# Head norms taken in the next head's turn, x loaded first, and latent attention with keys and values ahead of queries in the first pair

## The reference

```python
def hgrn_layer(h, mix, a, lb, w_in, g_out, w_out):
    q, f, i, g = jnp.split(h @ w_in, 4, axis=-1)
    ...
    o, S = mix(a, heads(jax.nn.silu(q)), heads(k), heads(i), heads(log_forget))
    o = rmsnorm(o, g_out.reshape(HG_HEADS, HG_DV)).reshape(Bn, T, -1).astype(h.dtype)
    return (o * jax.nn.silu(g)) @ w_out, S

# trunk, for each layer l
x = x + 0.5 * mods[:, 0, 2] * swiglu(mod(x, 0), w_ffn_gu[l, 0], w_ffn_down[l, 0])
y = hgrn_layer(...) if l == 0 else mla_layer(...)
x = x + mods[:, 1, 2] * y
x = x + 0.5 * mods[:, 2, 2] * swiglu(mod(x, 2), w_ffn_gu[l, 1], w_ffn_down[l, 1])
# before layer 1: ckv, krope = shared_kv(x, ...)
# mla_layer: qc = rmsnorm(h @ w_dq); q_lat, q_rope from qc; scores against ckv and krope; softmax; values; w_out
```

## Time and profile before

| what | before |
|---|---|
| median of 3 runs | 2585.49 us (2585.37 to 2586.11) |
| profiled execution: its own time, its span | 2586.55 us, 2585.0 us |
| busy share of the span: PE, PEld, DVE, ACT, POOL | 93%, 88%, 48%, 25%, 2% |
| mean granted clock of TensorE | 0.961 |
| head turns 0 to 6 (from 503.71 us to 807.60) | 303.9 us |
| last head (807.60 to 884.0) | 76.4 us |
| output projection (884.0 to 934.5) | 50.5 us |

### The profile page before, as it was taken

The page is one execution under the profiler, slowest core; times in us unless marked ns, Lnnn a source line. Parts: engine busy times, 40 slices in busy tenths (PEclk is TensorE's granted clock), DMA queues, the critical chain, the costliest instruction groups (busy, mean ns, idle before and its releaser), DMA issues.

```text
span 2585.0 us, 45686 instructions
## 1 busy us (share of the span) xinstructions
PE 2402.6 (93%) x19640; PEld 2270.4 (88%) x19640; DVE 1232.3 (48%) x2232; ACT 655.0 (25%) x810; POOL 53.9 (2%) x78
## 2 busy tenths in 40 slices
PE   5999999899997699999999999999787779999999
PEld 4999999898986599999998999998666459999998
DVE  4443344465657754434455443545554325543443
ACT  3222122222223122211233221123333223221213
POOL 2000000000000000000000000000000100000000
PEclk7999999899999699999999999999898989999999
DMA  7443452434333134434433443312112412323322
GB/s 258 164 163 111 136 164 81 145 116 132 115 132 107 34 114 165 146 100 151 133 98 123 158 150 102 98 62 71 63 38 90 167 78 82 98 70 101 91 73 74
DMA packets 317308, 294.42 MB, mean 114 GB/s; under 512 B 15597, under 2 KB 290116, under 8 KB 316144
## 3 DMA queue, kind: packets, MB, share of 16 engines
q1 hardware_dynamic: 310928, 260.41, 31.2%
q0 software_dynamic: 6240, 31.98, 3.3%
HBM read 284.83 MB, written 7.51 MB: 113 GB/s over the span
## 4 chain that ended last, share of the span: by engine, by line
PE 88%; DVE 6%; ACT 3%; issue 1%; DMA 1%; SPq 0%; DVEq 0%; ACTq 0%
PE ps L689 24%; PE ps L691 24%; PE ps L690 24%; PE ps L720 3%; PE ps L966 2%; PE ps L1252 1%; PE ps L1273 1%; ACT w_hi L1388 1%; DMA xs<-in_x_sample 1%; PE ps L1294 1%; DVE rstd L2107 1%; PE ps L1222 1%; PE ps L1203 1%; PE ps L1002 1%; DVE w_lo L1783 1%
## 5 line engine op out<-in xcount | busy, mean ns | idle before, releaser
L689 PE MATMUL ps<-hn_hi,w_hi 128*128 128x260 f32 (+1 forms) x2608 | 764.3, 293 | 14.1 <-DVE w_lo L1783 5.7
L691 PE MATMUL ps<-hn_hi,w_lo 128*128 128x260 f32 (+1 forms) x2608 | 747.8, 287 | 0.0
L690 PE MATMUL ps<-hn_lo,w_hi 128*128 128x260 f32 (+1 forms) x2608 | 747.6, 287 | 0.0
L1783 DVE TENSOR_TENSOR w_lo<-raw,w_hi 128x2048 fp32r<-128x2048 f32 (+5 forms) x200 | 381.0, 1907 | 345.0 <-ACT w_hi L1388 344.6
L689 PEld LDWEIGHTS ps<-hn_hi,w_hi 128*128 128x128 f32 x2608 | 500.5, 192 | 32.1 <-issue 23.6
L690 PEld LDWEIGHTS ps<-hn_lo,w_hi 128*128 128x128 f32 x2608 | 502.2, 193 | 0.1
L691 PEld LDWEIGHTS ps<-hn_hi,w_lo 128*128 128x128 f32 x2608 | 500.1, 192 | 0.0
L1388 ACT ACTIVATE w_hi<-raw 128x2048 fp32r<-128x2048 f32 (+4 forms) x193 | 319.0, 1654 | 578.4 <-DMA raw<-in_w_ffn_gu 378.0
L689 PE MATMUL ps<-hnb_hi,w_hi 128*128 128x260 f32 (+1 forms) x1456 | 415.5, 285 | 1.3 <-DVE zr L2189 0.9
L691 PE MATMUL ps<-hnb_hi,w_lo 128*128 128x260 f32 (+1 forms) x1456 | 414.8, 285 | 0.0
L690 PE MATMUL ps<-hnb_lo,w_hi 128*128 128x260 f32 (+1 forms) x1456 | 412.6, 283 | 0.0
(11 more groups left out here) (365 smaller groups left out, 2797.7 us busy)
## 6 DMA issues: line engine op xcount, KB each, us to landing
raw<-in_w_ffn_gu SPq DMA_DIRECT2D x176, 512.0 KB
raw<-in_w_ada SPq DMA_DIRECT2D x144, 512.0 KB
raw<-in_w_ffn_down SPq DMA_DIRECT2D x96, 384.0 KB
raw<-in_hg_w_in SPq DMA_DIRECT2D x32, 512.0 KB
raw<-in_w_ffn_down SPq DMA_DIRECT2D x32, 256.0 KB
raw<-in_kv_w_ada SPq DMA_DIRECT2D x16, 512.0 KB
ss<-in_state_hgrn POOLq DMA_DIRECT2D x8, 512.0 KB, 7.3
out<-ss POOLq DMA_DIRECT2D x8, 512.0 KB, 3.4
```

The lines of the kernel that those rows point to most:

```text
L689: pe.matmul(out, wh, xh[:, half], start=start, stop=False)
L690: pe.matmul(out, wh, xl[:, half], start=False, stop=False)
L691: return pe.matmul(out, wl, xh[:, half], start=False, stop=stop)
L1783: ins = dve.tensor_tensor(w_lo[r][:, c], raw[r][:, c], w_hi[:, r, c], ALU.subtract)
```

## The change

It has four parts.

**Start.** SP asks for `xs` and `xr` first, then the eight slabs. Constants and c come by ScalarE's queue. GpSimd waits until nine slots are used before it loads masks, page table and states. TensorE transposes x ahead of the first four slabs. ScalarE and VectorE do `scaled` ahead of the squares.

**HGRN2.** The norm of head n is put into head n+1's turn: `square` behind `finish` 1, `stat` ahead of level 7, the samples' sum inside `outs`, `invert` (reciprocal) behind tile 29, `apply` (scaling, gate, split) at the end. `LATE` goes from 26 to 28, `outs` ahead of `kt`, and `comb` right behind the turn's second slab. ScalarE's sigmoid of g moves to `finish` 3. At level 0 a multiplication by the identity replaces a memset and a predicated copy. The last head gets the norms of heads 6 and 7 alone, and, as its filling, half of the output projection (`first_out`: rows of heads 0 to 3, all eight output chunks); the other half follows (`second_out`). The slots of the output projection hold four row blocks by 512 outputs instead of eight by 256, and each chunk is added to x twice.

**Latent.** VectorE reads the first latent chunk after two `scaled` and the second after four.

**Latent attention.** Each operand gets its own semaphore (`qr_copied`, `q_copied[0]`, `q_copied[1]`, `kn_copied`, `ukt_copied`, `vh_copied`). A pair's order is queries (the rope chunk first), transposed key weights, keys, values, sample queries; in the first pair keys and values stand ahead of the queries. `vh` is waited for at the fourth step of the units. `dup` and a memset are made earlier, the scores of the new tokens come behind the first sample's scores, and a weight split moves from before the pages to behind them.

```diff
-LATE = 26
+LATE = 28
...
+    return (g("vt") + t(0, 3) + g("level", 0) + t(3, 3) + g("level", 1) + t(6, 3) + g("level", 2) + g("finish", 0)
+            + t(9, 3) + g("level", 3) + t(12, 2) + g("outer", 0) + t(14, 2) + ada(0) + g("level", 4) + g("finish", 1)
+            + norm("square") + t(16, 2) + g("level", 5) + t(18, 2) + g("outer", 1) + t(20, 2) + g("level", 6) + t(22, 2)
+            + norm("stat") + g("level", 7) + t(24, 2) + g("outs", normed) + g("kt") + t(26, 2) + g("state")
+            + t(28, 2) + norm("invert") + g("out") + t(30, 2) + ada(1) + comb + g("finish", 3) + norm("apply") + g("end"))
...
 def last_events():
+    t = lambda a, n: [("first_out", a, n)]
+    return (g("vt") + t(0, 2) + g("level", 0) + t(2, 2) + g("level", 1) + t(4, 2) + g("level", 2) + t(6, 2)
+            + g("level", 3) + t(8, 2) + g("outer", 0) + t(10, 2) + g("level", 4) + g("square", 1) + t(12, 2) + g("level", 5)
+            + t(14, 2) + g("ada", 2) + g("outer", 1) + t(16, 2) + g("level", 6) + t(18, 2) + g("stat") + g("level", 7)
+            + g("outs", True) + t(20, 2) + g("kt") + t(22, 2) + g("state") + g("invert") + g("out") + g("apply")
+            + t(24, 2) + g("end") + g("square", 2) + t(26, 2) + g("stat") + g("stats") + g("invert") + g("apply", 2) + t(28, 4)
+            + g("ada", 3) + g("comb"))
...
@@ SP
+            sp.dma_start(xs[:], a["x_sample"].rearrange("b s d -> (b s) d")).then_inc(s_xin, 16)
+            for t in range(4):
+                sp.dma_start(xr[:, t, :], a["x_prompt"][0, t * P:(t + 1) * P, :]).then_inc(s_xin, 16)
...
@@ GpSimd
+            pool.wait_ge(slot_used, ADA_S * ADA_FIRST + 1)
             pool.dma_start(lmask[:], a["level_masks"]).then_inc(s_tab, 16)
...
@@ TensorE
+            def second_out():
+                for c in range(2):
+                    for k in range(4, 7):
+                        out_tile(c, k, 4)
+                pe.wait_ge(head_hi, H)
+                for c in range(2):
+                    out_tile(c, 7, 4)
+                for c in range(2, KD):
+                    for k in range(4, KD):
+                        out_tile(c, k, 4)
...
+                    elif kind == "stat":
+                        pe.wait_ge(head_sq, T.at("ns", 1))
+                        out, done = att()
+                        pe.matmul(out, ones[:], s1[:, 0:NP], start=True, stop=True).then_inc(done, 1)
...
             pe.wait_ge(lat_done, 2)
...
+            for hp in range(4):
+                if hp:
+                    queries(hp)
+                keys(hp)
+                head_values(hp)
+                if hp == 0:
+                    queries(hp)
+                sample_queries(hp)
...
@@ ScalarE
+                    elif kind == "finish" and j == 3:
+                        act.wait_ge(g_read, T.at("proj", 1))
+                        act.wait_ge(q_ready, T.at("proj", 1))
+                        act.nop(nofuse=True)
+                        act.activation(sgx.unsqueeze(1), gg[:, bass.ds(hn, 1), :], ACT.Sigmoid, bias=bcol[:, 4:5]
+                                       ).then_inc(act_part, 1)
...
@@ VectorE
+                    elif kind == "invert":
+                        dve.wait_ge(head_root, T.at("ns", 1))
+                        dve.reciprocal(s2[:, 0:NP], s2[:, 0:NP])
+                    elif kind == "apply":
+                        n = h if j == 2 else h - 1
+                        dve.wait_ge(head_root_s, T.at("ns", 1))
+                        link(dve.reciprocal(s2[:, NP:NT], s2[:, NP:NT]))
+                        link(dve.tensor_tensor(s1[:].unsqueeze(1), og[:, head, :], s2.unsqueeze(1), ALU.mult))
+                        link(dve.scalar_tensor_tensor(s1[:].unsqueeze(1), s1[:].unsqueeze(1), vec[:, bass.ds(n + V_HG, 1)],
+                                                      gg[:, head, :], ALU.mult, ALU.mult))
+                        split_act(s1[:].unsqueeze(1), o_hi[:, head, :], o_lo[:, head, :], head_hi)
...
+            for c in range(2):
+                scaled(c, hnb_hi, hnb_lo)
+            latent(0, z[:, 0, :], 0)
+            for c in range(2, 4):
+                scaled(c, hnb_hi, hnb_lo)
+            latent(1, z[:, 1, :], 1)
```

More of the change, by code:

```diff
@@ L144, in last_events @@
-def last_events():
-    events, out, h = hgrn_events(False), [], 0
-    for e in events:
-        out.append(e)
-        if e[0] in ("level", "outer") and h < H - 1:
-            out.append(("norm", h, 0))
-            h += 1
-    return out + [("norm", n, 0) for n in range(h, H + 1)]
+    ada = lambda j: g("ada", slab + j)
+    norm = lambda kind: g(kind) if normed else []
+    comb = g("comb") if slab == ADA_S - 2 else []
+    return (g("vt") + t(0, 3) + g("level", 0) + t(3, 3) + g("level", 1) + t(6, 3) + g("level", 2) + g("finish", 0)
[3 more added lines that the diff above has]
+            + t(28, 2) + norm("invert") + g("out") + t(30, 2) + ada(1) + comb + g("finish", 3) + norm("apply") + g("end"))
@@ L950, in hgrn_step @@
                         ada_comb()
+                    elif kind == "stat":
+                        pe.wait_ge(head_sq, T.at("ns", 1))
+                        out, done = att()
+                        pe.matmul(out, ones[:], s1[:, 0:NP], start=True, stop=True).then_inc(done, 1)
+                        T.add("ns")
+                    elif kind == "stats":
+                        out, done = att()
+                        pe.matmul(out[:, 0:NS], ones[:], s1[:, NP:NT], start=True, stop=True).then_inc(done, 1)
                     elif kind == "vt":
@@ L1130, in _, with queries @@
             pe.wait_ge(lat_done, 2)
-            for hp in range(4):
+            def queries(hp):
                 hi, lo = slabs(QK, 384)
@@ L1482, in out_projection, with second_out @@
                 T.add("res", KD)
+            def second_out(xh):
+                for c in range(KD):
+                    if c % 4 == 0:
+                        split_hi()
+                        T.add("slot")
+                    x_square(c, updated(c))
+                    scaled(c, xh)
+                T.add("res", KD)
             def hgrn_step(events, q, h):
@@ L1967, in ffn, with out_chunk, second_out @@
                     add_mods(due)
+            def out_chunk(c):
+                if c % 4 < 3:
+                    T.add("part")
+                    residual(c, c % 2, (o_part, T.n["part"]))
+                else:
+                    residual(c, 1)
+                    T.add("slot")
+                if c == KD - 1:
+                    T.add("res", KD // 2)
+            def second_out(*following):
+                modulation(*following)
+                xh, xl = following[2:]
+                for c in range(KD):
+                    if c % 4 == 0:
+                        split_lo()
+                    out_chunk(c)
+                    if c % 2 == 0:
+                        if c:
+                            prepared(c - 1, xh, xl)
+                        prepared(c, xh, xl)
+                scaled(KD - 1, xh, xl)
             def out_projection(gate_base, *following):
@@ L2151, in _ @@
             factors(C_L0, V_NORM)
-            for c in range(KD - 1):
-                add_square(c)
             for c in range(KD):
```

486 lines of the change are left out of this document (257 added, 229 removed).

## The result

The changed kernel takes **2527.14 us** (median of 4 runs, 2526.22 to 2529.55) against 2585.43 for the kernel before on the same chip: a ratio of 0.9777, with a 95% interval of 0.9760 to 0.9794. The forecast was 2535 and the range 2511 to 2556; the gain is 58.3 us where 50.4 were forecast.

What follows compares the result with a forecast made beforehand. TensorE, 88% busy, was taken as the bound, so only its waits and half clock pay. Seven parts (-11.5, -2.4, +15, -33, -6, -11, -1.5) sum to -50.4 us from 2586.55: 2536.2, as median 2535, range 2511 to 2556.

Steps and rivals of the forecast that it cites:

- part 1: Start: x asked for first and splits ahead of squares, -11.5 us, ends -8 and -14.
- part 3: Head turns 0 to 6: state waits removed, but norm work and level-1 waits added, +15 us, ends -8 and +30.
- the -20.2: Head turns: six waits for head-state copies removed, -12.8 us, and four half-clock spells behind them, -7.4.
- part 2: Projection into head 0: two small waits, for rows and a split, go, less 0.4: -2.4 us.
- part 4: Last head and output projection: six norms leave and projection tiles fill the levels' gaps, 126.9 to 94, -33 us.
- The ends: Last head and projection: outer bounds, 75 us (work and a third of the waits) and 112 (half the gain).
- Rival B: Last head stays VectorE's, leaving TensorE 112 us there: 2553 us in all, chance 0.20.
- rival A: Head turns: VectorE keeps up, no level-1 waits or half clock behind them: 2510 us in all, chance 0.20.
- parts 5 to 7: Shared latent -6 us, latent attention -11 and pages -1.5, from waits removed or shortened.
- The 10.0-us wait: Latent attention: first pair's keys do not hide the wait for the second latent; nothing counted.
- part 6: Latent attention: three waits of every pair and half clock behind them go, -11 us, ends -5 and -14.
- Rival C: Head turns' clock falls to the last head's 0.68, +100 us: 2620 us or more, chance 0.04.

Runs made afterwards that it cites:

- the hold alone: Kernel before with only GpSimd's loads held until nine slots are used: 2577.3 us; the changed kernel without that hold: 2536.3 us.
- the order of squares: Changed kernel with x's squares put ahead of x's splits at the start again, as in the kernel before: 2528.1 us.
- Late split alone: Kernel before with LATE at 28 alone, so VectorE copies the head state ahead of the weight split: 2564.9 us.
- the first pair's wait: Changed kernel with the wait for the second latent moved from ahead of the first pair's keys to behind its values: 2521.1 us.
- the pages' split: Changed kernel with the pages' weight split in the last sample's waits instead of ahead of the final denominators: 2527.6 us.
- apply first: Changed kernel with the rest of the norm (`apply`) ahead of the gate's product (`finish` 3) instead of behind it: 2513.4 us.
- sum earlier: Changed kernel with `apply` ahead of `finish` 3 and the norm's sum (`stat`) ahead of level 6 instead of level 7: 2497.5 us.
- reciprocal early: Changed kernel with the norm's reciprocal (`invert`) behind `outs` and ahead of `kt`, instead of behind the weight split: 2515.0 us.
- without table loads: Changed kernel with the square roots of the turns' head norms replaced by a scaling that needs no table: 2508.6 us.
- the last one: Changed kernel with `stat`, reciprocal and `apply` moved, first pair's keys and values early, and the page split moved: 2484.2 us.

## Why the prediction held, and where its steps did not

**Start (part 1): the size was right, the reason was not.** The prediction gave the gain to x ahead of the slabs and to the splits ahead of the squares, and booked the loads held back at GpSimd as worth nothing, or as a cost of up to 2. The runs turn that round: the hold alone is worth 8.1 us in the kernel before and 9 in the changed one, the order of squares nothing that these runs can tell (+0.9 us in a spread of 6.7), and some 2 to 3 of the 11.5 us are left for x first and the start's other edits, which were not tried by themselves. The prediction's times for the changed start came out (first pair at 38.2, measured 38.67), because they were reckoned as if no other load were in the way; that the price of those loads was put at nothing did not show in the sum, and that is luck. The step that failed is the sentence that drew from the Trainium skill's rule on shared engines (DMA: Bandwidth & Descriptors, "Issuing engines are not separate DMA queues") that the bytes are only paid later. The engines are shared, and the trace agrees: slabs two to four started 4 to 8 us later beside these loads. But the delay was about twice what the bytes explain (above), and nobody waits for the bytes when they do land: the last wait for a transfer in the changed kernel's table of TensorE's waits ends at 31.3 us, and the loads are asked for from 56.4 on. The row that was at hand, slab four's wait of 2.8 us, was read as a bound on the gain; it was a sign of the cause.

**Turns (part 3): the mechanism and its sizes were right.** The five waits at level 1 were to be 13.4 us and were 13.4; `outs` was to wait 0.7 and waited 0.5 to 0.7; `comb` 0.8 and 0.7. Late split alone confirmed the -20.2. Of +15 forecast 11.5 came, and turn 0 is the difference: it got back 7.8 us, not one wait and a spell (4.0), for the half clock at its start had been put at nothing and the wait of 1.0 there counted in part 2. The six turns with a norm came out at +19.3, as the same terms give. In them the spells' sum was right by luck: 9.5 forecast, and 8.8 by the granted clock of turns 1, 3 and 5 (0.96, 0.96, 0.90). They were taken as one of 1.9 behind each level-1 wait. Behind the 2.3-us waits there was none, behind the 3.3-us waits one each, and two stood behind `outs`, in turns 1 and 5.

**Last head (part 4): mis-sized by 5.** Of the waits, level 1 was forecast 5.0 and measured 5.0, the norm of head 7 2.6 and 2.6, the output 2.1 and 1.5, levels 2 and 5 3.0 and 1.7. The second half of the projection was to wait 10.6 and waited 3.7, one of them 3.1 for a chunk's sum that stood behind a split. There the prediction put every split and chunk sum in series ahead of TensorE; in the trace VectorE still has idle time between chunks. In all 15.0 us of waits came for 24.4. Half clock took some 7 us, not 4.7. By these terms it is 65 + 15 + 7 = 87, measured 88.0. (The ends, by the prediction's own words, would be 73 and 110 rather than 75 and 112.) Rival B is out with the 88.0, and rival A with the waits at level 1.

**Latents and pages (parts 5 to 7): right in kind.** These parts, and part 2, were read from the traces; of them only the first pair's wait and the pages' split were tried by themselves. The third chunk's wait fell from 5.54 to 0.41, and the wait at the next ffn rose from 0.86 to 1.78 with a half-clock spell behind it, forecast 2. The 10.0-us wait stayed, as said; of the 12.9 us of part 6, 1.4 lie ahead of the pairs. The pages lost 3.4 rather than 1.5: the first page transpositions now run at full clock, which the sum had left out, while the final wait rose from 3.2 to 5.1.

Rival C, the clock in all turns, did not come: the windows above stand at 0.90 to 1.00. Still, the clock and not the waits themselves is the larger part of the 16 us that apply first left and sum earlier won.

## What to carry to other kernels

When work is moved into the shadow of another engine, write out the moved engine's chain in series between the two hand-overs that matter and compare it with the other engine's work between the same two points; here that gave the wait to a tenth of a microsecond, and showed the two swaps that remove it. At a program's start, ask of every load in flight who waits for it next; those that nobody needs should not be asked for yet, on any queue. And a short wait ahead of matmuls of few columns can cost more than its length, since the clock may fall behind it; look at the granted clock there, and not only at the wait.

## What the hardware showed that was not expected

In apply first and reciprocal early the granted clock fell to one half behind a wait of 0.5 to 0.7 us followed by 1.9 us of one-column matmuls, in six turns of six (reciprocal early, 610 to 615 us: 0.66 with TensorE busy throughout). In the changed kernel the same waits and matmuls stand in the same six turns, and the clock fell behind them in turns 1 and 5 only; turns 4 and 6 above stayed at 1.00. It did not fall behind the same matmuls without the wait (sum earlier), nor behind waits of 2.0 us (without table loads) and 2.3 us (changed kernel) at level 1, and it fell behind the waits of 3.3. Which pieces of idle time and narrow work add up to a fall is not settled by these runs.

The runs of one kernel spread more where such spells are in it, 2509.1 to 2518.3 us for reciprocal early and 2483.7 to 2485.0 for the last one; but the kernel without table loads spreads from 2504.5 to 2512.7, and the trace of its fastest execution has none in the turns, so this is a hint only.

With small loads in flight on GpSimd's queue the 16 DMA engines moved a third to a half of what they move without them, 129 and 202 GB/s for 400 and 405, and stood partly idle. Which of the loads does it was not tried.
